# Delta rule layer: q, k, v of groups 1 to 7 and z of all groups by seven products per pair of tiles

## The reference, cut to what matters

```
def branch_inputs(u):                       # u: [tokens, 1024], context and latent apart
    p = u @ w_in
    qkv = silu(centred_dwconv(p[..., :4096], conv_w))      # 5 taps, zero padding
    z = p[..., 4096:6144]
    q, k, v = split(qkv, [1024, 2048])      # 8 heads q, k; 16 heads v; head width 128
    q, k = l2_norm(q), l2_norm(k)
    ...
def chunk_gated_delta(...):                 # per head, both directions
    a = strict_lower(k_beta k^T * decay); t_inv = inverse(I + a)
    ...  scan over chunks: state, output o
def finish(o, z):
    o = rms_norm(o, o_norm_g)
    return (o * silu(z)) @ w_out
```

## Time and profile before

| | us |
|---|---|
| median of 3 runs | 2926.69 |
| the runs | 2927.52, 2923.0, 2926.69 |
| the profiled execution | 2928.49 |
| its span | 2926.7 |
| PE busy | 2800.1 (96%) |
| DVE busy | 1446.7 (49%) |
| ACT busy | 978.7 (33%) |
| POOL busy | 249.6 (9%) |

### The profile page before, as it was taken

The page is one execution under the profiler, slowest core; times in us unless marked ns, Lnnn a source line. Parts: engine busy times, 40 slices in busy tenths (PEclk is TensorE's granted clock), DMA queues, the critical chain, the costliest instruction groups (busy, mean ns, idle before and its releaser), DMA issues.

```text
span 2926.7 us, 39634 instructions
## 1 busy us (share of the span) xinstructions
PE 2800.1 (96%) x16306; PEld 1972.7 (67%) x16306; DVE 1446.7 (49%) x2980; ACT 978.7 (33%) x2531; POOL 249.6 (9%) x172
## 2 busy tenths in 40 slices
PE   8899999999999999999999989999999999999998
PEld 3677778787777867664645335578677664688886
DVE  3466574756657464633334244533357321677732
ACT  1436455463636544003234123322223311211200
POOL 0000000000000000000000022113112220000031
PEclk9999999999999999999999999999999999999999
DMA  5101111110111232502100001112132111221220
GB/s 224 46 10 49 61 22 45 23 45 22 50 29 49 79 109 98 201 29 93 58 29 22 31 23 72 58 58 86 73 115 87 43 72 58 95 89 61 99 103 29
DMA packets 76341, 193.74 MB, mean 66 GB/s; under 512 B 56096, under 2 KB 60960, under 8 KB 64512
## 3 DMA queue, kind: packets, MB, share of 16 engines
q1 hardware_dynamic: 52720, 181.92, 17.0%
q10 hardware_dynamic: 23440, 9.28, 1.2%
HBM read 181.22 MB, written 9.96 MB: 65 GB/s over the span
## 4 chain that ended last, share of the span: by engine, by line
PE 89%; ACT 6%; DVE 4%; issue 1%; DMA 1%; SPq 0%; DVEq 0%; ACTq 0%
PE ps L1722 9%; PE ps L1922 9%; PE ps L1190 8%; PE ps L1247 7%; PE ps L1285 6%; PE ps L1469 5%; PE ps L1950 4%; PE ps L1248 4%; PE ps L1739 3%; PE ps L1862 3%; ACT arena L1979 2%; PE ps L1600 2%; PE ps L1328 2%; PE ps L1338 2%; PE ps L1299 2%; PE ps L1350 2%
## 5 line engine op out<-in xcount | busy, mean ns | idle before, releaser
L1979 ACT ACTIVATE arena<-ps 64x64 f32<-64x64 f32 (+7 forms) x1011 | 327.0, 352 | 766.8 <-PE ps L1722 164.1
L1722 PE MATMUL ps<-arena 128*128 128x256 f32 x1456 | 327.6, 379 | 2.0 <-ACT arena L1979 2.0
L1722 PEld LDWEIGHTS ps<-arena 128*128 128x128 f32 x1456 | 270.6, 190 | 40.1 <-issue 5.7
L1247 PE MATMUL ps<-arena 128*128 128x512 f32 x512 | 263.8, 597 | 1.7 <-DVE arena L2629 1.7
L1922 PE MATMUL ps<-arena 128*128 128x256 f32 x1176 | 254.5, 378 | 0.0
L1922 PEld LDWEIGHTS ps<-arena 128*128 128x128 f32 x1176 | 222.2, 189 | 32.6 <-issue 0.5
L1190 PE MATMUL ps<-arena 128*128 128x512 f32 x496 | 222.4, 608 | 14.7 <-DVE arena L2985 5.1
L1190 PEld LDWEIGHTS ps<-arena 128*128 128x128 f32 x496 | 95.9, 194 | 139.6 <-issue 130.3
L1980 ACT ACTIVATE arena<-ps,arena 128x128 f32<-128x128 f32 x544 | 156.6, 381 | 86.1 <-PE ps L1403 45.7
L1248 PEld LDWEIGHTS ps<-arena 128*128 128x128 f32 x512 | 97.2, 190 | 124.5 <-issue 124.5
L1285 PE MATMUL ps<-arena 128*128 128x256 f32 x768 | 178.0, 385 | 0.0
(11 more groups left out here) (351 smaller groups left out, 4294.2 us busy)
## 6 DMA issues: line engine op xcount, KB each, us to landing
arena<-in_ada_w SPq DMA_DIRECT2D x12, 2048.0 KB, 9.6
arena<-in_w_up SPq DMA_DIRECT2D x11, 2048.0 KB, 8.1
arena<-in_w_dil SPq DMA_DIRECT2D x9, 2048.0 KB, 8.0
arena<-in_w_dn SPq DMA_DIRECT2D x8, 2048.0 KB, 10.2
arena<-in_w_gate SPq DMA_DIRECT2D x6, 2048.0 KB, 8.0
arena<-in_w_down SPq DMA_DIRECT2D x4, 2816.0 KB, 9.6
arena<-in_att_in SPq DMA_DIRECT2D x5, 2048.0 KB, 8.1
arena<-in_w_z SPq DMA_DIRECT2D x8, 1024.0 KB, 4.9
```

The source lines that it names most:

```text
L1247: e.matmul(ps[:, b1, :], w, uT[:, k * T_ALL + 256:(k + 1) * T_ALL], start=k == 0, stop=k == 7)
L1722: m = e.matmul(ps[:, bank, 0:256], left[:, k], right[:, k], start=first and k == 0, stop=k == 3, skip_group_check=not first)
L1979: return e.activation(out, x, ACT.Copy)
```

## The change

- For groups 1 to 7 the four tiles are taken as two pairs (p = 0: q, k; p = 1: the two v heads), and z of every group as a third pair (p = 2). A pair is made by seven products of 4 matmuls with 385 columns each: two halves of the contraction, two tiles, two halves of the tokens. Tokens are padded to 770 (two zero columns between context and latent). Group 0's q, k, v stay as they were (`PROJ0`).
- PE: P1, P6, P7 and P4 accumulate one on the other in bank a; after each ACT copies the bank out (`pair_snap`), and the next may start once that is read. P2 and P3 use bank c, P5 bank b; DVE adds them into the tile in SBUF (`pair_add`).
- POOL makes four sums of weights per pair into one buffer `S_dn`, each waiting for the product of the pair before that read its quarter, and once, at the start, three sums of the activations (and one in place). POOL's multiply of z with `o_norm` goes; that factor is now in `fin_y` on DVE, which takes the turned output from PSUM and multiplies by the feature-major z, in place of `gated` (DVE) and ACT's copy. SP sends the result.
- The taps of group k move from before the joins to the joins, SiLU of the v tiles (`silu`, j, 2, 3) from the joins to the start of the next round, right behind `zg`, and `turn` of the v tiles from the joins to before the joins, behind `solved` (for group 7 both stay behind the last join step). Products of pairs 0 and 1 of group k stand before the joins, those of z of group j in the joins.
- Buffers: six rotating `conv_buf` for `raw` and `cv`; the ring's slot 1 holds q, k, v, slot 0 z.

```diff
@@ dn_order, one round, j < 7
+            zh = [x for name in SEVEN for x in unit(j, 2, name)]
...
         yield "clean", j
         if j:
             yield "zg", j - 1
-        early = {3: 4, 5: 5, 8: 6, 10: 7, 12: 8, 14: 9}
...
+        if j < 7:
+            yield "silu", j, 2, 3
+            yield from unit(k, 0, "P2") + unit(k, 0, "P6")
+            if j:
+                yield "sum_sq", j - 1
+            yield "pair_add", k, 0, "P2"
+            yield from unit(k, 0, "P5")
+            yield "pair_add", k, 0, "P5"
+            if j:
+                yield "gate_o", j - 1
+            yield from unit(k, 0, "P7")
+            yield "pair_add", k, 0, "P7"
+            yield "blocks", j
+            yield from unit(k, 0, "P3")
+            yield "solve", j, 1
+            yield "pair_add", k, 0, "P3"
+            yield from unit(k, 0, "P4")
+            if j:
+                yield "finish", j - 1
+            for i in range(2, 9):
+                yield "solve", j, i
+            yield from unit(k, 1, "P1") + unit(k, 1, "P2") + unit(k, 1, "P6")
+            for i in range(9, 16):
+                yield "solve", j, i
+            yield from unit(k, 1, "P5")
+            yield "solved", j
+            yield "pair_add", k, 1, "P2"
+            if j:
+                yield "fin_y", j - 1
+            yield "turn", j, 0
+            yield "turn", j, 1
...
+            t = [x for n in range(4) for x in conv(k, n)]
+            behind = [zh[:2] + t[:5], zh[2:4] + t[5:6], z_add("P2") + zh[4:7] + t[6:12],
+                      [("silu", k, 0, 1)] + z_add("P5") + zh[7:10] + z_add("P7") + t[12:14], zh[10:12] + t[14:15],
+                      z_add("P3") + zh[12:] + t[15:] + [("norm_sq", k, 0)],
+                      [("norm", k, 0), ("norm_x", k, 0), ("norm_sq", k, 1)], [("norm", k, 1), ("norm_x", k, 1)], []]
+            if k == 7:
+                behind[8] = [("silu", 7, 2, 3), ("turn", 7, 0), ("turn", 7, 1)]
@@ PE
+                bank, left, right, n, first, event = {
+                    "P1": (a, a_[:, 0], U_H[:, 0, :, 0], None, True, "snap1"),
+                    "P2": (c, a_[:, 1], U_H[:, 1, :, 0], None, True, "c11"),
+                    "P6": (a, s[1], T2, 1, False, "snap2"),
+                    "P5": (b, s[0], T1, 0, True, "c22"),
+                    "P7": (a, s[2], T3, 2, False, "snap3"),
+                    "P3": (c, s[3], U_H[:, 1, :, 1], 3, True, "c12"),
+                    "P4": (a, b_[:, 1], T4, None, False, "c21")}[name]
...
+                    take_banks(bank)
+                for k in range(2 * part, 2 * part + 2):
+                    m = e.matmul(ps[:, bank, 0:HALF_PAD], left[:, k], right[:, k], start=first and k == 0, stop=k == 3,
...
+                    leave_banks((f"pair_{event}", j, p), bank)
@@ POOL, per pair
+                e.wait_ge(*pair_landed(j, p))
+                free("P5")
+                e.tensor_tensor(s[0], b_[:, 0], b_[:, 1], ADD).then_inc(*mark("pair_s", j, p, 0))
...
@@ DVE
+                e.scalar_tensor_tensor(o1, t[:, :, 256:768], V("o_norm"), g[:, :, 258:770], MUL, MUL)
+                e.scalar_tensor_tensor(o2, t[:, :, 0:256], V("o_norm"), g[:, :, 0:256], MUL, MUL).then_inc(*mark("y", j))
```

More of the change, by code:

```diff
@@ L23 @@
     "mod": "mod sc mu0",
[L24 removed]
+    "dn": "proj raw pads tap conv silu nrm turn v kn z pair osum osq ored orstd onrm fin y",
     "inv": "inv solve solved spread clean unit0 unit",
@@ L267, in conv, with unit @@
         return [("conv", j, n, q) for q in range(first, last)]
-    def gate(j, i, banks=(0, 1)):
-        return [("z", j, c, part, banks[i % 2]) for c in (2 * i, 2 * i + 1) for part in range(4)]
-    def beside(one, other):
-        return [x for both in itertools.zip_longest(one, other) for x in both if x]
+    def unit(j, p, name):
+        return [("pair", j, p, name, part) for part in range(2)]
     def norms(j, n):
@@ L2239, in scalar_program @@
                     kn(*which)
-                elif what == "z":
-                    j, c, part, b = which
-                    if c % 2 and part == 3:
-                        z(j, c, b)
+                elif what == "pair":
+                    if which[3]:
+                        pair_snap(*which[:3])
                 elif what == "zg":
@@ L2280, in scalar_program @@
                     sum_sq(*which)
-                elif what == "finish":
-                    finish(*which)
             for n in range(8):
@@ L2862, in vector_program @@
                     gate_o(*which)
+                elif what == "fin_y":
+                    fin_y(*which)
+                elif what == "pair_add":
+                    pair_add(*which)
             def slab_sums(n):
```

399 lines of the change are left out of this document (231 added, 168 removed).

## The result

| | median | lowest to highest | profiled execution | span | mean granted clock |
|---|---|---|---|---|---|
| before | 2927.1 us | 2923.0 to 2929.8 | 2928.5 us | 2926.7 us | 0.989 |
| after | 2992.2 us | 2988.7 to 2997.0 | 2990.0 us | 2988.2 us | 0.973 |

A forecast was written before the change was run, and what follows sets the result against it. PE's own work was taken to bound the kernel. Six rounds of 5.9 - 1.4 = 4.5 us (+27), +6.5 for round 6, -1 for group 7 and 0 for round 0 gave +33, so 2960 us; range 2915 to 2993.

The forecast's parts named there:

- What bounds it: Whole kernel: PE's own work sets the time (busy 96% of the span); DVE, ACT and DMA steps are hidden behind it.
- the wait of P7: Before the joins: P7 waits for ACT's copy of P6, behind four table loads and SiLU; 7.6 us of idle PE.
- the wait of the second turn: Before the joins: the second turn waits on DVE's chain of solve, fin_y and copy; 1.6 us late.
- the waits in the joins: In the joins: PE waits for DVE's norm_sq of k, 2.4 us; the stretch as a whole changes by -1.4 us.
- the forecast's 98: Whole kernel: 98 us of waiting put in, against 65 us of work taken from PE, for +33.
- the sentence on the clock: All three stretches of a round: the granted clock is full (1.00), so the change can't gain there; no size.
- the 65 us that PE saves: PE work over the whole kernel: 7 x 8.7 + 3.7 for z of group 7 = 65 us saved.
- Round 0, "0, within 5": Round 0: POOL's sums and P7's wait against z parts that come into the joins; change 0, within 5 us.
- Round 6 and group 7, "+6.5" and "-1": End of round 6: SiLU of two tiles and the turns uncovered, +6.5 us; group 7: less PE work, -1 us.
- POOL, "0.7 before the joins, 1.5 in the joins": Each round: POOL's 12 weight sums slow DVE, costing the path 0.7 us before the joins and 1.5 in them.
- The rival of the table loads: ACT: a drain of 1.4 us on each of four loads makes 5.5 us per round, 2993 us; chance 3%.
- The PE saving: PE work per round: 21 products of 54.4 us against some 63, saving about 8.7 us.

The follow-up runs named there:

- the two fillings: Changed kernel with idle PE products added: in P7's wait (2982.2 us), then also in the waits of k's norm and the scan's first step (2971.7 us).
- the last run: Changed kernel with idle PE products in P7's wait, and four more each in the waits of k's norm and the scan's first step; 2971.7 us, ratio 1.0151.
- first: Against the changed kernel: SiLU of the two v tiles moved from ahead of ACT's copy of P6 to behind its copy of P4; 2964.2 us, ratio 1.0123.
- second: Against the first run's kernel: SiLU of z also moved, behind ACT's copy of the blocks; 2931.3 us, ratio 1.0011.
- fourth run: Against the changed kernel: 16 idle PE products put between P5 and P7 in groups 2 to 7, nothing moved; 2982.2 us, ratio 1.0190.
- The last kernel: Against the twelfth run's kernel: sum of k's norm behind join y of 64, DVE's scaling of k behind the scan's first v step; 2884.6 us, ratio 0.9851.
- the eighth run: Against the seventh run's kernel: sum of k's norm behind the join y of 64 instead of ahead of it; 2914.8 us, ratio 0.9955.
- fifth run: Against the second run's kernel: DVE squares q one join step earlier, and squares k before it scales q; 2913.5 us, ratio 0.9951.
- seventh: Fifth run's kernel with the second turn behind P7, fin_y behind the first turn's copy; in group 7, zg behind the blocks' copy, finish later; 2893.7 us.
- twelfth: Against the seventh run's kernel: SiLU of v of group 7 moved behind z's last product in the joins of round 6; 2888.2 us, ratio 0.9868.

## Why the prediction was half right

- **What bounds it, the wait of P7, the wait of the second turn, the waits in the joins: right.** Forecast 7.6, 1.6, 2.4 us; the trace has 7.64, 1.67, 2.28, and 90 us of added idle time in all for the forecast's 98. With the waits filled, a round takes 134.1 against the forecast's 134.7.
- **The step that failed** is the sentence on the clock: "The clock granted is full (1.00) in all three, and the change can't gain there." It asked only whether there was something to gain. It should have asked what the change could lose: in the kernel before PE waits 1.22 us at the longest in the rows of a round, and the forecast itself put 7.6 us of idle into it. Measured price: 10.0 us behind P7's wait, 10.5 behind the other two (the two fillings), 20.5 in all, where 32 us were missing.
- **In the sum, the clock's price stood at nothing, and so the 65 us that PE saves came out too large.** The work is gone, but part of what is left runs at half clock: PE's busy time fell by 28.5 us, 36.5 short of 65. In windows of 0.5 us from 100 to 1300 us, PE is busy at the half clock for 9.6 us in the kernel before, 73.2 in the changed one and 22.6 in the last run. A product of 385 columns takes 982 ns there and 483 at the full clock, so half of such time is lost: 4.8, 36.6 and 11.3 us. That is an estimate, since some of it may hide in waits; the 31.8 us between the two kernels are all but the 32 that were missing.
- **Round 0, "0, within 5": +10.7, too small.** Before, the joins of group 0 lasted 44.0 us, 6.9 less than later ones, as 8 parts of z stood ahead of them. After, all of z is in the joins, and the stretch ahead had to become shorter to pay for it. It did not: from 120 us to the first join step PE had 52.6 us of work in place of 59.9, but idled 13.3 in place of 6.2, and the granted clock was 0.87 in place of 0.97. Work at half clock ahead of the first join step costs 4.4 us more than before, by the estimate above. POOL's sums of tokens are worth 3 us at most by their run; without the weight sums too the first join step began at 180.0. In that execution the clock had also been higher ahead of this stretch (1.00 in 100 to 120 us for 0.91), but so it had in the last run, which began its joins at 185.9. How the rest divides between POOL and ACT's late copies stays open: in the runs with POOL's sums whole the first join step lies anywhere from 184.0 to 188.8, so smaller parts can't be told here.
- **Round 6 and group 7, "+6.5" and "-1": together +14.5, 9 too small.** At the end of round 6 PE idled 3.4, 4.8 and 1.1 us with the turns at half clock between (1.54 us each for 0.88). In group 7 `finish` stood 7.6 us behind DVE's gate, which the forecast had no term for. Moving the two gave 5.7 and 5.3 back. About 7 us of the stretch are lost at half clock, by the estimate above, where the kernel before loses next to nothing. In the first, second and fourth run, which left the stretch alone, it takes 142.4 to 143.1 us against 140.4 here, so the 9 are known to some 3 us only.
- **POOL, "0.7 before the joins, 1.5 in the joins"**: 13 us by that, 7.7 measured, more than half of it ahead of the first join step. In the plain rounds its 2.2 us each were far too dear: without the weight sums they are 0.1 to 0.5 us shorter.
- **The rival of the table loads** gave 2993, and the time came out at 2992, but it is wrong: in the time line of ACT each operation starts within 0.02 us of its load's end, and P7's wait is 7.64 with no drain in it. The Trainium skill's drain of 1.38 us ("ScalarE: Activation LUTs", What ACT_TABLE_LOAD costs) does not show here. A time that fits is no proof of a mechanism.
- **The PE saving** is real. With the steps reordered the round takes 121.7 to 123.1 us, against 130.2 before: 7 to 8.5 of the forecast's 8.7 us.

The last kernel, the changed one in another order of its steps, takes 2884.6 us and is faster than the kernel before by 1.5% (ratio 0.9851), and than the changed one by 108 us. Between it and its neighbour at 2888.2 the intervals overlap. The change itself was sound; the order of its steps, on ACT above all, lost more than it brought.

## What to carry to other kernels

When a change puts an idle stretch into a PE-bound stage, count the wait and then a second price for the clock behind it. Here that price did not follow the length of the wait: 1.7 us behind 3.28 in each round, 1.35 to 3.0 behind 7.64, 3 behind the 3.27 of the eighth run, and 0 or 1.7 behind 2.02. So halving a wait need not halve its price; taking it away, or filling it, does away with both. Work that another engine may do at any time within a round (an activation with its table loads) belongs behind the copies that PE waits for, and a step that waits for another engine's result belongs behind what the next stage needs from the same queue. And where work is moved from one stretch into the next, as z was in round 0, check that the first one really becomes shorter.

## What the runs showed of the hardware

TensorE's granted clock falls to its lower level (1.2 GHz) in or just behind a stretch in which PE idles, and comes back some 3 to 6 us into the new work: behind 7.64 us of idling it was 0.53 already before PE went on; behind 3.28 it was still 1.00 when PE went on and 0.50 within 1 us. The Trainium skill, "TensorE: Matmul & The Clock Gate", Part 1: The HAM clock gate, says that the low clock is the default and that activity lifts it; the runs agree, since idle products that compute nothing of use brought 20.5 us.

Behind a single wait of 2.02 us it is not the same in each round. The clock in the scan's first 4 us, for the six scans with this wait, was 0.57 to 0.62 in three and 1.00 in three (fifth run), 0.57 or 0.58 in five and 1.00 in one (seventh), three and three in the twelfth. Behind waits of 1.67 (the second turn), 1.26 and 1.22 us it stayed at 1.00 in the stretches read. The forecast had no means to price this, and a difference of a few us between such kernels may be no more than that.
